# Three 256-column matmuls into one set of columns in place of a 512- and a 256-column matmul

## What is computed

```python
for layer in range(2):
    shift, scale, gate = split(silu(c) @ ada_w[layer, 0] + ada_b[layer, 0], 3)
    hn = rmsnorm(x, norm_g[layer, 0]) * (1 + scale) + shift
    y = rglru_mlstm_mixer(hn, ...) if layer == 0 else stick_breaking_mixer(hn, ...)
    x = x + gate * y
    shift, scale, gate = split(silu(c) @ ada_w[layer, 1] + ada_b[layer, 1], 3)
    hn = rmsnorm(x, norm_g[layer, 1]) * (1 + scale) + shift
    x = x + gate * ((silu(hn @ w1[layer]) * (hn @ w3[layer])) @ w2[layer])
return rmsnorm(x, final_g)
```

## Time and profile before

| | |
|---|---|
| median of 3 runs | 2453.87 us |
| the profiled execution's own time | 2454.73 us |
| its span, first to last instruction | 2453.0 us |
| mean granted TensorE clock | 0.983 |
| TensorE matmuls busy | 2266.0 us (92%), 12638 matmuls |
| TensorE weight loads busy | 1956.7 us (80%), 12638 loads |
| DVE busy | 1887.5 us (77%) |
| ACT busy | 1028.7 us (42%) |
| POOL busy | 245.9 us (10%) |
| HBM read | 616.80 MB, 252 GB/s over the span |

### The profile page before, as it was taken

The page is one execution under the profiler, slowest core; times in us unless marked ns, Lnnn a source line. Parts: engine busy times, 40 slices in busy tenths (PEclk is TensorE's granted clock), DMA queues, the critical chain, the costliest instruction groups (busy, mean ns, idle before and its releaser), DMA issues.

```text
span 2453.0 us, 36210 instructions
## 1 busy us (share of the span) xinstructions
PE 2266.0 (92%) x12638; PEld 1956.7 (80%) x12638; DVE 1887.5 (77%) x2347; ACT 1028.7 (42%) x1183; POOL 245.9 (10%) x209
## 2 busy tenths in 40 slices
PE   0289998989999999999989999998999999999998
PEld 0277887778888888888878888887888888888887
DVE  7888897988887888778896666678887566666667
ACT  1134456344433443344455455534443344433443
POOL 6100000510000000000240000033000000000014
PEclk9989998999999999999999999999999999999999
DMA  8798775867777776777756655665776555555554
GB/s 345 292 377 312 280 282 210 308 236 282 282 271 286 279 285 270 287 277 289 280 215 272 243 222 219 244 241 212 301 276 255 188 189 188 188 188 188 188 201 159
DMA packets 86186, 619.80 MB, mean 253 GB/s; under 512 B 10216, under 2 KB 10472, under 8 KB 10984
## 3 DMA queue, kind: packets, MB, share of 16 engines
q1 hardware_dynamic: 85248, 617.79, 65.7%
q10 hardware_dynamic: 872, 1.15, 0.1%
HBM read 616.80 MB, written 2.10 MB: 252 GB/s over the span
## 4 chain that ended last, share of the span: by engine, by line
PE 83%; DVE 10%; issue 3%; POOL 2%; ACT 1%; DMA 0%; DVEq 0%; POOLq 0%; ACTq 0%
PE ps L962 49%; PE ps L960 12%; PE ps L965 12%; PE ps L934 4%; DVE adaw L585 3%; DVE wlow L577 3%; PE ps L911 2%; POOL work L381 1%; POOL work L375 1%; PE ps L913 1%; DVE raw L585 1%; ACT whigh L415 1%; DVE work L703 1%; PE ps L1085 1%; DVE hn L709 0%
## 5 line engine op out<-in xcount | busy, mean ns | idle before, releaser
L415 ACT ACTIVATE whigh<-raw 128x1024 fp32r<-128x1024 f32 x784 | 828.0, 1060 | 1182.5 <-PE ps L962 1113.7
L577 DVE TENSOR_TENSOR wlow<-raw,whigh 128x1024 fp32r<-128x1024 f32 x784 | 974.3, 1261 | 391.3 <-ACT whigh L415 382.6
L962 PE MATMUL ps<-hn,whigh 128*128 128x512 f32 x3712 | 1174.6, 397 | 5.1 <-DVE wlow L577 5.1
L962 PE MATMUL ps<-mid,whigh 128*128 128x512 f32 x1856 | 588.0, 397 | 8.5 <-DVE wlow L577 8.5
L962 PEld LDWEIGHTS ps<-hn,whigh 128*128 128x128 f32 x3712 | 569.1, 189 | 7.2 <-issue 6.8
L960 PE MATMUL ps<-hn,wlow 128*128 128x256 f32 x1856 | 517.7, 279 | 0.0
L965 PE MATMUL ps<-hn,wlow 128*128 128x256 f32 x1856 | 515.9, 278 | 0.0
L960 PEld LDWEIGHTS ps<-hn,wlow 128*128 128x128 f32 x1856 | 349.5, 188 | 85.0
L965 PEld LDWEIGHTS ps<-hn,wlow 128*128 128x128 f32 x1856 | 350.3, 189 | 79.6
L585 DVE CUSTOM_DVE_ANT_0 adaw<-adaw,cact 128x2048 f32<-128x2048 f32 x176 | 407.1, 2316 | 5.8 <-DMA adaw<-ada_dram 5.6
L962 PEld LDWEIGHTS ps<-mid,whigh 128*128 128x128 f32 x1856 | 284.9, 189 | 12.2 <-DVE wlow L577 7.6
(11 more groups left out here) (197 smaller groups left out, 1243.6 us busy)
## 6 DMA issues: line engine op xcount, KB each, us to landing
raw<-wts_dram SPq DMA_DIRECT2D x392, 1024.0 KB, 4.8
adaw<-ada_dram SPq DMA_DIRECT2D x176, 1024.0 KB, 6.7
raw<-ada_dram SPq DMA_DIRECT2D x16, 1024.0 KB, 5.6
x<-xT_dram SPq DMA_DIRECT2D x1, 2048.0 KB, 13.9
out_dram<-x SPq DMA_DIRECT2D x4, 512.0 KB, 2.6
cact<-c_row_dram SPq DMA_DIRECT2D x1, 1024.0 KB, 5.1
work<-lru_w_dram ACTq DMA_DIRECT2D x1, 1024.0 KB, 6.6
mod<-ada_b_dram SPq DMA_DIRECT2D x1, 96.0 KB, 4.3
```

The source lines that it names most:

```text
L415: act.activation(whigh[:, (2 * s + h) % 4, :], raw[:, s, h * HALF:(h + 1) * HALF], ACT.Copy)\
L577: dve.tensor_tensor(wlow[:, half, :], raw[:, s, h * HALF:(h + 1) * HALF], whigh[:, half, :].bitcast(F32), ALU.subtract).then_inc(S["low_re ...
L962: ins = pe.matmul(ps[:, s, :], whigh[:, half, w], src[:, kk, :, :], start=kk == 0, stop=kk == kts - 1, skip_group_check=True)
```

## The change

For each contraction tile the three products are now three matmuls of 256 columns into the same lower half of the bank: `whigh` with the high part, `whigh` with the low part, `wlow` with the high part, in that order for every `k`. Each has its own weight load. So a bank's result stands complete in 256 columns, and every eviction is one operation: in `up` bodies ACT takes Silu straight from PSUM for even s, and for odd s DVE multiplies it with the PSUM columns; the two reductions are gone. In `out` and `down` bodies one operation adds gate times the result to `x`. In `STORED` bodies DVE alone writes the scaled result, and ACT's copy is gone. The semaphores `half_added`, `half_stored` and `hidden_product` are gone. In `up` bodies the product counts `chunks_evicted` up by two, and DVE no longer waits at even s.

```diff
@@ ScalarE, body
-                    if kind in STORED:
-                        first, tiles, number, numbers, factor = STORED[kind]
+                    if kind[:2] == "up" and s % 2 == 0:
                         act.wait_ge(S["halves_multiplied"], n * 8 + 2 * s + 2 + CREDIT)
-                        dst = work_tile(i * tiles + (first + s))
-                        act.activation(dst, ps[:, s, T:2 * T], ACT.Copy, scale=factor)\
-                           .then_inc(S["half_stored"], 1)
-                    if kind[:2] == "up" and s % 2:
-                        act.wait_ge(S["chunks_evicted"], n * CH + s + CREDIT)
-                        act.activation(work[:, 2 + s // 2, :], work[:, s // 2, :], ACT.Silu).then_inc(S["silu_ready"], 1)
+                        act.wait_ge(S["chunks_evicted"], n * CH + s + CREDIT - 2)
+                        act.activation(work[:, 2 + s // 2, :], ps[:, s, 0:T], ACT.Silu).then_inc(S["silu_ready"], 1)
@@ VectorE, update_x
-                tmp = work[:, 8 + s, :]
                 xm = x[:, m, :].rearrange("p a t -> p (a t)")
-                dve.scalar_tensor_tensor(tmp, ps[:, s, 0:T], gate, xm, ALU.mult, ALU.add).then_inc(S["half_added"], 1)
-                dve.wait_ge(S["half_added"], count + 1)
-                dve.scalar_tensor_tensor(xm, ps[:, s, T:2 * T], gate, tmp, ALU.mult, ALU.add).then_inc(S["chunks_evicted"], 1)
+                dve.scalar_tensor_tensor(xm, ps[:, s, 0:T], gate, xm, ALU.mult, ALU.add).then_inc(S["chunks_evicted"], 1)
@@ VectorE, body
-                    dve.wait_ge(S["halves_multiplied"], n * 8 + 2 * s + 2 + CREDIT)
+                    if not (kind[:2] == "up" and s % 2 == 0):
+                        dve.wait_ge(S["halves_multiplied"], n * 8 + 2 * s + 2 + CREDIT)
                     if kind in STORED:
-                        dve.wait_ge(S["half_stored"], i * numbers + (number + s + 1))
-                        dve.scalar_tensor_tensor(dst, ps[:, s, 0:T], factor, dst, ALU.mult, ALU.add).then_inc(S["chunks_evicted"], 1)
+                        dve.tensor_scalar(work_tile(i * tiles + (first + s)), ps[:, s, 0:T], factor, None, ALU.mult)\
+                           .then_inc(S["chunks_evicted"], 1)
...
-                        if s % 2 == 0:
-                            sum_halves(work[:, j, :], s)
-                            units_of(pair, units, s)
-                        else:
+                        units_of(pair, units, s)
+                        if s % 2:
...
-                            sum_halves(work[:, 4 + j, :], s)
-                            units_of(pair, units, s)
                             dve.wait_ge(S["silu_ready"], count + 1)
+                            dve.tensor_tensor(work[:, 6 + j, :], work[:, 2 + j, :], ps[:, s, 0:T], ALU.mult)\
+                               .then_inc(S["chunks_evicted"], 2)
                             dve.wait_ge(S["chunks_evicted"], n * CH + s + 1 + CREDIT)
-                            dve.tensor_tensor(work[:, 6 + j, :], work[:, 2 + j, :], work[:, 4 + j, :], ALU.mult)\
-                               .then_inc(S["hidden_product"], 1)
-                            dve.wait_ge(S["hidden_product"], count + 1)
@@ TensorE, fresh_half
-                        pe.matmul(ps[:, s, :], whigh[:, half, w], src[:, kk, :, :], start=kk == 0, stop=False,
-                                  skip_group_check=True)
-                        ins = pe.matmul(ps[:, s, T:2 * T], wlow[:, half, w], src[:, kk, 0, :], start=False,
-                                        stop=kk == KT - 1, skip_group_check=True)
+                        for last, a, part in ((False, 0, whigh), (False, 1, whigh), (True, 0, wlow)):
+                            ins = pe.matmul(ps[:, s, 0:T], part[:, half, w], src[:, kk, a, :], start=kk == 0 and part is whigh and a == 0,
+                                            stop=last and kk == KT - 1)
@@ TensorE, body
-                            if k % 2:
-                                pe.matmul(ps[:, s, T:2 * T], wlow[:, half, w], src[:, kk, 0, :], start=False, stop=False,
-                                          skip_group_check=True)
-                            ins = pe.matmul(ps[:, s, :], whigh[:, half, w], src[:, kk, :, :], start=kk == 0, stop=kk == kts - 1,
-                                            skip_group_check=True)
-                            if k % 2 == 0:
-                                pe.matmul(ps[:, s, T:2 * T], wlow[:, half, w], src[:, kk, 0, :], start=False, stop=False,
-                                          skip_group_check=True)
+                            for last, a, part in ((False, 0, whigh), (False, 1, whigh), (True, 0, wlow)):
+                                ins = pe.matmul(ps[:, s, 0:T], part[:, half, w], src[:, kk, a, :],
+                                                start=kk == 0 and part is whigh and a == 0, stop=last and kk == kts - 1)
```

More of the change, by code:

```diff
@@ L62 @@
 LAST_UPDATE = [None, OUT0, FFN0 + FFN_BODIES - DOWN, OUT1, BODIES - DOWN]
-UPDATES = {"out0": 0, "down0": KT, "out1": KT * 4, "down1": KT * 5}
 STORED = {"qk": (0, 4, 0, 4, 1.0), "o": (8, 4, 8, 4, 1.0), "x_branch": (16, 4, 16, 4, 1.0),
@@ L214, in bass_trunk @@
         names = """c_loaded norm_consts_loaded x_loaded small_loaded lru_w_loaded stored
-            high_ready low_ready halves_multiplied chunks_evicted half_added half_stored
+            high_ready low_ready halves_multiplied chunks_evicted
             unit_done mod_added c_ready consts_ready pick_ready
@@ L218, in bass_trunk @@
             hn_high_ready hn_ready final_ready
-            silu_ready hidden_product hidden_high hidden_ready
+            silu_ready hidden_high hidden_ready
             gate_w_high gate_w_ready lam_abs lam_exp lam_ready
@@ L598, in units_of @@
                     add_unit(adaw[:, u % 2, :], u, pair * 2)
[L600 to L604, removed]
             def update_x(n, s, kind, q, i):
                 norm = {"out0": 0, "down0": 1, "out1": 2, "down1": 3}[kind]
-                count = q * KT + i * CH + UPDATES[kind] + s
                 m = bass.ds(i * CH + s, 1)
```

## The result

The changed kernel takes 2504.54 us in the median of 4 runs (2500.59 to 2506.3), the kernel before 2453.74 beside it: a ratio of 1.0205, 95% interval 1.0187 to 1.0222. It is 50.8 us slower where 24 us faster was forecast, and above the range. The profiled execution took 2500.59 us.

A forecast was written before the change was run, and what follows sets the result against it. TensorE's streaming of matmuls was taken to bound the kernel. Matmuls -11.7 us and evictions -12.3 us sum to -24 us from the profiled 2454.7, forecast 2430 us, with a range of 2405 to 2490 us.

The forecast's parts named there:

- What bounds the kernel: FFN stretches of layers 0 and 1: TensorE, busy all 100 us with 576 matmuls in each, sets the pace.
- below 862: Sign of a wrong prediction: fewer matmuls than this per 100 us of pure streaming, where 867 were forecast.
- The matmuls: Ordinary chunks: three 256-column matmuls at 115.4 ns make a tile 346.2 ns instead of 348.3; times 5568, -11.7 us.
- a third in a row finds what the second found: Loads start with the matmul ahead, none earlier, so a third 256-column matmul in a row also costs 115.4 ns.
- The bound from above: Dearest distances with a 256-column matmul are 0.12 us; at a 119 ns pitch a tile costs 357 ns, +48 us.
- two rows at 111 ns: Eight matmuls with 128-column loads, and four loads with single-column matmuls: taken as a load's pitch, 111 ns.
- Rival 2: Every chunk: the third load competes with streaming, 119 ns instead of 111; +36 us, 2490 us; chance 20%.
- Rival 1: Cutting the long matmul costs what it saves: TensorE gives 0 to +14 us, middle 2449 us; chance 17%.
- rival 3: A pure stream goes at the loads' pitch, 112 ns, 336 ns a tile; -80 us, 2374 us; chance 8%.
- The fixed 2.5 ns: Skill's fixed cost per matmul: three short ones would be 2.5 ns a tile dearer, +14 us instead of -12; set aside.
- The evictions: Shorter evictions in `up`, `out` and `down` bodies: -2.8 - 7.5 - 2.0 = -12.3 us, between -2 and -16.

The follow-up runs named there:

- runs_of_eight: Kernel before, with eight 512-column matmuls, then eight 256-column ones, in each half of a chunk instead of two and two; 2465.44 us, ratio 1.0048.
- half_moving: Changed kernel, streaming only 128 of 256 activation columns in every ordinary-chunk matmul but the first of a bank; 3435.93 us.
- the size runs: Four versions of the changed kernel: 64 or 96 weight columns, 128 or 192 streamed columns in most matmuls; 2412.40, 2440.98, 3435.93 and 2380.50 us.

## Why the prediction was wrong

**What bounds the kernel** was read rightly: streaming by TensorE, with the count of matmuls per 100 us as the measure. The count of the changed kernel, 835 where below 862 was to be the sign of a wrong forecast, shows the miss.

**The step that failed** is the price of 115.4 ns in "The matmuls", and its size: 120.0 in a pure stream. 3 x 4.6 ns x 5568 = +77 us, which is the 74.5 us between the forecast 2430 and the measured 2504.5, but for 2 us. The faulty inference was that "a third in a row finds what the second found", drawn from the start stamps of the loads. Nearly all of these lie 2 to 5 ns behind the start of the matmul ahead, in the kernel before as in the changed one, so they cannot show slack. The single stamps of runs_of_eight show what the pairs hid: 114, then 119, then 120. A pair behind two long matmuls, with mean 115.4, is the part of a run that is still fast.

**The bound from above** was 119 ns from "0.12" in the timeline; the stamps behind it were 112 and 119 in turn. As a bound it was 1 ns short. It was given too little chance, for two rows at 111 ns spoke against it, and these were rows of another kind in the point that mattered: a load beside 128 columns of float32 or beside a single column, while ours stands beside 256 columns of float32r. With 128 weight and 128 streamed columns, half_moving gives the same 110.5 ns. The price of a load was right beside a short stream, and I took it for a load beside a whole one.

**Rival 2** is what happened, with its place (every chunk), its condition (no long matmul between the short ones; the load is slower beside a whole stream) and nearly its price: at 120 ns it gives +65.1 - 12.3, 2506.7 us, 2 us over the measured. It had 20%.

**Rival 1** (a part of the long matmul's price that stays) would need 116 ns, rival 3 112; both fall with 120. The fixed 2.5 ns that the Trainium skill gives ("TensorE: Matmul & The Clock Gate", "Back-to-back issue gap") hold there for a matmul by itself and not for a stream of load and matmul pairs, whose spacing both set; the prediction used them without that condition. They would have made the loss an estimated 2.5 ns a tile, and the trace has 11.7: the right sign and a fifth of the size. The same page of the Trainium skill says ("Step-by-step: what each phase is for") that loading the next weights does not take read bandwidth from the running matmul. The runs do not show what is shared, so they do not bear on bandwidth as such; but 120.0 ns with both at full length and 114.3 and 110.5 with one of them halved show that the two are not independent in this kernel.

**The evictions** were right in size, with some luck: -12.3 forecast, -13.4 measured alone, of which 7.3 us are the waits that were to shrink, and most of the rest goes with a higher granted clock. In the changed kernel the waits are near the forecast: for `wlow` 5.5 us (some 6 forecast), for hidden tiles 3.7 (4.6). Beside the slower matmuls the evictions give only some 7 to 9 us. Why is not shown: these waits shrink there from 18.3 to 9.2 us, by more than at the old pace.

**What stays open.** Which resource load and stream share is not shown: the size runs say that both sizes matter, and neither in proportion. Nor is it shown why a 512-column matmul costs 226 to 241 ns according to its neighbours, or what picks one of two paces. One thing narrows it down: at half the granted clock the effect is gone (last section).

## What to carry to other kernels

If a change makes longer runs of one kind of matmul, take the price from a run as long as the new one: a pair behind a long matmul cost 115.4 ns here, a stream 120. If two things overlap, take the price with both at full length; with one of them shorter it was 3 to 10 ns too low here. Where TensorE streams, one 512-column matmul with one load beats two of 256 with two (232.9 ns against 240 here), even at the cost of a longer eviction on another engine. Where that other engine sets the pace, the opposite holds, and a kernel may well use both forms, each in its own stage.

## What the runs showed of the hardware

**The clock of half_moving.** With 128 weight and 128 streamed columns TensorE's clock stood at the lower of its levels, 1.2 GHz, in long stretches in which TensorE issued one matmul behind the other. Four stretches, the third at full clock:

```profile
700.00:800.00 100.00, 99.08 (x830) 98.94 (x829) 71.89 (x84) 37.90 (x41) 0.00 (x0) 0.93 0.74 276
786.60:1810.60 1024.00, 1020.08 (x4781) 1019.64 (x4781) 419.38 (x479) 231.36 (x247) 30.25 (x32) 0.50 0.41 157
2300.00:2406.00 106.00, 106.00 (x949) 105.86 (x947) 79.64 (x92) 44.09 (x50) 0.00 (x0) 1.00 0.77 292
2500.00:2600.00 100.00, 100.00 (x470) 100.00 (x470) 28.14 (x30) 20.83 (x22) 0.00 (x0) 0.50 0.29 105
```

At a granted clock of 0.50 there are 470 matmuls in 100 us, 213 ns each, so a kernel that computes half as much took 3435.93 us. The clock fell at 786.6 and at 2407.9 us, each time 1.0 to 1.5 us behind a wait of TensorE (the wait stands in brackets):

```profile
785.08 0.44 PE L941 MATMUL ps<-mid,whigh 128*128 128x128 f32 x2 [0.92 <-DVE mid L641]
2406.94 0.44 PE L941 MATMUL ps<-mid,whigh 128*128 128x128 f32 x2 [0.94 <-DVE mid L641]
```

Two more of the five long falls (at 400.9 and 465.8 us) stand behind waits of 0.99 and 0.97 us; the fifth (301.9) has no such wait before it but eight matmuls of four rows. Between 2300 and 2406 us the same matmuls kept a clock of 1.00. Once down, the clock stayed down for 1024 us although TensorE was shown as busy for 1020 of them, and it rose at 1810.6 amid matmuls of 256 columns (L892). The kernel before waited longer at such a place, and its clock stayed at 1.00:

```profile
701.22 0.39 PE L960 MATMUL ps<-mid,wlow 128*128 128x256 f32 x1 [1.33 <-DVE mid L661]
```

With 192 streamed columns it stayed at 1.00 in the stretches read, with matmuls as close together.

**At half the clock the change costs nothing.** The changed kernel has short stretches at a granted clock of 0.50, one of them from 307.1 to 310.5 us:

```profile
307.95 0.63 PE L939 MATMUL ps<-hn,whigh 128*128 128x256 f32 x2
...
309.87 0.63 PE L939 MATMUL ps<-hn,whigh 128*128 128x256 f32 x2
```

Nine distances in 1.92 us are 213 ns each, and in the kernel before a 512-column matmul takes 427 and a 256-column one 213 or 214 at this clock: 640 ns a tile in both. The distance is 213 ns as well with 64 weight columns, and with 128 streamed columns in half_moving. So at half the clock load and stream, both whole, take no longer together than with one of them halved. Half of 213 would be an estimated 107 ns at full clock, where 110.5, 114.3 and 120.0 were measured: what is added there does not go with TensorE's clock.
